# Scores of the samples: even and odd head pairs in different column halves of TensorE

## The reference

```python
logits = jnp.einsum('bthd,btjhd->bthj', q, kg, preferred_element_type=jnp.float32) * ATTN_SCALE
logits = jnp.where(valid[None, :, None, :], logits + bias[None, None], -jnp.inf)
m = jnp.max(logits, axis=-1, keepdims=True)
pr = jnp.exp(logits - m)
den = jnp.sum(pr, axis=-1)
o = jnp.einsum('bthj,btjhd->bthd', pr, vg.astype(jnp.float32)) / den[..., None]
```

## Time and profile before

| what | value |
|---|---|
| median of three runs | 2098.59 us |
| profiled execution | 2098.7 us |
| its span | 2096.9 us |
| mean granted clock of TensorE | 0.987 of 2.4 GHz |
| TensorE busy | 1998.9 us, 95% |
| VectorE busy | 1031.3 us, 49% |
| ScalarE busy | 699.6 us, 33% |
| GpSimd busy | 941.6 us, 45% |

### The profile page before, as it was taken

The page is one execution under the profiler, slowest core; times in us unless marked ns, Lnnn a source line. Parts: engine busy times, 40 slices in busy tenths (PEclk is TensorE's granted clock), DMA queues, the critical chain, the costliest instruction groups (busy, mean ns, idle before and its releaser), DMA issues.

```text
span 2096.9 us, 30132 instructions
## 1 busy us (share of the span) xinstructions
PE 1998.9 (95%) x11992; PEld 1820.7 (87%) x11992; DVE 1031.3 (49%) x1355; ACT 699.6 (33%) x1194; POOL 941.6 (45%) x580
## 2 busy tenths in 40 slices
PE   8999999988888999899999999999999999999999
PEld 7999998777777888565567799999999999999998
DVE  4888803877767666477777561521212212121212
ACT  5344323666556676555552021210010101010010
POOL 4688613777657665234332123233332323232332
PEclk9999999999999999999999999999999999999999
DMA  4444435453343442878755423011111111111112
GB/s 168 149 190 160 149 113 127 115 121 101 87 112 95 117 132 81 267 258 277 232 210 191 172 99 126 31 51 41 51 40 50 40 50 41 49 40 50 40 50 93
DMA packets 117925, 239.36 MB, mean 114 GB/s; under 512 B 29995, under 2 KB 63659, under 8 KB 116284
## 3 DMA queue, kind: packets, MB, share of 16 engines
q1 hardware_dynamic: 94956, 205.69, 30.4%
q10 hardware_dynamic: 22864, 32.25, 4.7%
HBM read 187.78 MB, written 58.67 MB: 118 GB/s over the span
## 4 chain that ended last, share of the span: by engine, by line
PE 65%; DVE 7%; ACT 6%; issue 4%; POOL 1%; DMA 0%; ACTq 0%; DVEq 0%; SPq 0%; POOLq 0%
PE wo_psa L2377 9%; PE wo_psa L2395 9%; PE wo_psb L2377 9%; PE wo_psb L2395 7%; PE dense_ps L966 6%; PE wo_psa L2225 4%; PE sa_s L1512 3%; PE wo_psb L2329 2%; PE wo_psa L2329 2%; DVE att_p L1071 1%; PE att_t_ps L995 1%; ACT att_p L1165 1%; PE ssd_in L1616 1%; PE att_s_ps L984 1%; ACT att_qhi L1182 1%
## 5 line engine op out<-in xcount | busy, mean ns | idle before, releaser
L913 POOL TENSOR_SCALAR att_p<-att_p,att_rden 128x128 f32<-128x128 f32 (+7 forms) x128 | 251.0, 1969 | 132.6 <-DVE att_rden L1053 132.6
L2134 POOL CAST wo_hi<-wo_raw 128x1024 fp32r<-128x1024 f32 x64 | 66.7, 1042 | 496.8 <-issue 242.1
L2492 ACT ACTIVATE r_sq<-stage 128x1056 f32<-128x1056 f32 x32 | 34.8, 1089 | 625.1 <-DVE stage L2693 625.1
L2136 POOL TENSOR_TENSOR wo_lo<-wo_raw,wo_hi 128x1024 fp32r<-128x1024 f32 x64 | 185.3, 2895 | 5.1
L1058 DVE TENSOR_TENSOR att_pTlo<-att_t_ps,att_pThi 128x512 fp32r<-128x512 f32 x192 | 106.3, 554 | 112.1 <-ACT att_pThi L1173 110.6
L2377 PE MATMUL wo_psb<-mix_split,wo_hi 128*128 128x352 f32 x768 | 144.9, 323 | 0.0
L2377 PE MATMUL wo_psa<-mix_split,wo_hi 128*128 128x352 f32 x768 | 144.2, 322 | 0.0
L1173 ACT ACTIVATE att_pThi<-att_t_ps 128x512 fp32r<-128x512 f32 x192 | 93.4, 487 | 127.9 <-PE att_t_ps L995 120.7
L966 PE MATMUL dense_ps<-u_hi,w_hi 128*128 128x352 f32 x480 | 117.8, 347 | 16.4 <-DVE conv_pre L1085 7.8
L2377 PEld LDWEIGHTS wo_psb<-mix_split,wo_hi 128*128 128x128 f32 x768 | 128.3, 188 | 0.5 <-issue 0.5
L2377 PEld LDWEIGHTS wo_psa<-mix_split,wo_hi 128*128 128x128 f32 x768 | 128.0, 188 | 0.0
(11 more groups left out here) (315 smaller groups left out, 5148.0 us busy)
## 6 DMA issues: line engine op xcount, KB each, us to landing
sa_k<-in_cache_k SPq DMA_DIRECT2D x32, 640.0 KB, 7.6
sa_v<-in_cache_v SPq DMA_DIRECT2D x40, 512.0 KB, 4.7
w_raw<-in_w_feat SPq DMA_DIRECT2D x36, 512.0 KB, 6.3
wo_raw<-in_w_up SPq DMA_DIRECT2D x32, 512.0 KB, 3.5
wo_raw<-in_w_down SPq DMA_DIRECT2D x32, 512.0 KB, 3.5
out_qk<-proj_out SPq DMA_DIRECT2D x16, 528.0 KB, 7.9
tmp_bias_rows<-tmp_table ACTq DMA_DIRECT2D x8, 1024.0 KB
att_bias<-tmp_bias_rows SPq DMA_DIRECT2D x16, 512.0 KB, 3.2
```

What stands on the lines that cost most here:

```text
L913: pool.tensor_scalar(slot(h, qt), slot(h, qt), rden[:, qt, :], None, ALU.mult).then_inc(normed, 1)
L2136: pool.tensor_tensor(w_lo[:, j], raw_w, w_hi[:, j].bitcast(F32), ALU.subtract).then_inc(f_split[j], 1)
```

## The change

The two pairs of a group go to different partitions of the same two banks: the even one to partitions 0 to 63 as before, the odd one to 64 to 127. The order within a group becomes columns outside, pairs inside: even 512, odd 512, even 160, odd 160. Each half of the partitions is its own accumulation, begun by the first group's pair and closed by the last group's. VectorE adds the two: first the odd half and the bias go to `probs`, then the old instruction takes the even half and `probs`, writes the sum back and keeps the minimum. `biased` counts twice a sample, and its three waits change with it. Number and size of the matmuls and of the weight loads stay the same.

```diff
-                for i in range(KP):
-                    f = u * KP + i
-                    for c, w in ((0, 512), (512, NKEYS - 512)):
-                        mm = pe.matmul(s_ps[0:R, c:c + w], q_diag[:, f, :], kT[:, u, i, c:c + w],
-                                       start=(f == 0), stop=(f == NPAIR - 1))
+                for c, w in ((0, 512), (512, NKEYS - 512)):
+                    for i in range(KP):
+                        f = u * KP + i
+                        mm = pe.matmul(s_ps[i * R:(i + 1) * R, c:c + w], q_diag[:, f, :], kT[:, u, i, c:c + w],
+                                       start=(f < KP), stop=(f >= NPAIR - KP))
                 mm.then_inc(k_used, 1)
...
-                    pool.wait_ge(biased, b)
+                    pool.wait_ge(biased, 2 * b)
...
-                act.wait_ge(biased, b + 1)
+                act.wait_ge(biased, 2 * b + 2)
...
-                dve.tensor_tensor_reduce(out=probs[:, 0:NKEYS], in0=s_ps[0:R, 0:NKEYS], in1=bias[:], scale=1.0, scalar=3e38,
-                                         op0=ALU.add, op1=ALU.min, accum_out=low[:]).then_inc(biased, 1)
+                dve.tensor_tensor(probs[:, 0:NKEYS], s_ps[R:2 * R, 0:NKEYS], bias[:], ALU.add).then_inc(biased, 1)
+                dve.wait_ge(biased, 2 * b + 1)
+                dve.tensor_tensor_reduce(out=probs[:, 0:NKEYS], in0=s_ps[0:R, 0:NKEYS], in1=probs[:, 0:NKEYS], scale=1.0,
+                                         scalar=3e38, op0=ALU.add, op1=ALU.min, accum_out=low[:]).then_inc(biased, 1)
```

## The result

The changed kernel takes 2110.84 us (median of 12 runs, 2096.31 to 2121.31), the kernel before beside it 2098.51 us (median of 12). The ratio is 1.0054, with an interval of 1.0030 to 1.0078: slower, by 0.3 to 0.8%. The forecast of 2096.8 us said no change, and its range ended at 2107. The profiled execution took 2110.1 us, its span is 2108.3. Over the twelve runs the time goes with the mean granted clock: the fastest of them had 0.982, the slowest 0.972.

What follows compares the result with a forecast made beforehand. The prediction took TensorE (PE), busy 95%, as the bound, with VectorE deciding after the change. Samples 2 to 7 gain 6 x 0.15 = 0.9 us, sample 1 gains 1.0: 1.9 off 2098.7 gives 2096.8 us, range 2092 to 2107.

Steps and rivals of the forecast that it cites:

- step 4: `states(n,1)` on PE, samples 2 to 7: waits for VectorE until 935.24, 0.16 early; afterwards all follows PE, 0.15 us arrive.
- The clock: Rival, chance 0.05: PE's new idle time in the mixers lowers the clock to 1.2 GHz, 1.2 us a sample, 2107.
- the sign of being wrong: Period of samples 2 to 7 moving by more than 0.6 us from 29.2, or score groups staying at 2.40 us.
- Overlap: Score matmuls on PE: even and odd halves run side by side, a group takes 1.75 us, gaining 0.65.
- The sum over 1.56: Score group's halves on PE: only neighbours of unlike parity pair up, 0.43 + 0.43 + 0.43 + 0.27 = 1.56 us.
- The add: VectorE's new instruction before the minimum: 0.85 us plus 0.03 wait, 0.88; hidden in sample 0, not in samples 1 to 7.
- the first rival: No overlap, chance 0.19: PE gains nothing, VectorE's add makes `states(n,1)` 0.46 late, 7 x 0.46 = 3.2, 2101.9 us.
- Step 2: VectorE before y's second turn: GpSimd's earlier decay holds `mix(n,2)`, run ends 0.37 later, turn 0.62 early instead of 1.95.
- Steps 3 and 4: VectorE's new add puts `add_state(n,0)` at 935.17 for 934.91; `states(n,1)` waits for it; 0.15 us a sample arrive.
- A reading: Mixers' stage before the change: the windows of samples 1 to 6 are 29.2 us each.
- PE's gain arrives: Rival, chance 0.07: VectorE isn't in the way of PE's faster scores, 7 x 2.6 = 18.2 us gained, 2080.4.

Runs made afterwards that it cites:

- experiment 3: The change with matmuls of constants filling PE's idle time: two before y's second turn, one each before second state update and first score group, six at stage start; 2095.65 us, 0.9973.
- experiments 5: The change with only some of experiment 3's fillers: rounds only 0.9964, start only 1.0047, second turn of y only 1.0113, second state update only 0.9993.
- experiment 6: The kernel before, matmuls untouched, with three redundant VectorE adds (672, 672 and 256 columns) ahead of the minimum; 2138.35 us, ratio 1.0166.
- experiment 1: The kernel before with one redundant VectorE add ahead of the minimum; 2105.02 us, ratio 1.0016.
- experiment 8: experiment 3 with one filler instead of two at y's second turn, and GpSimd's state decay held until VectorE is through `split_v(n,1)`; 2088.76 us, ratio 0.9947.
- experiment 7: The change with three of four `split_v` moved on VectorE's list behind what PE waits for, 2077.29 us, 0.9881; the same list in the kernel before, 2102.32 us, 1.0001.
- experiment 4: The change with the old order within a score group, pairs outside and columns inside; 2112.17 us, ratio 1.0039.

## Why the prediction was wrong

**The step that failed** is the last half sentence of step 4, "From there all follows PE", which took PE at 2.4 GHz to the end of the sample. It was the rival "The clock", with a chance of 0.05 and 1.2 us a sample. In the seven rounds it took 16 us (219.0 against experiment 3's 203.0), 2.3 a round, and they are 31.3 us on the mean for 29.2, beyond the 0.6 that the prediction itself set as the sign of being wrong. Its "Against" was the error: gaps of 1.32 us at 1.00 were read as if a gap's length told all. The gap at the first score group and the one at the second state update are of like length; the second follows the short matmuls of `inner`, and it alone brings the long falls, in most rounds that have it (experiments 5, 6). That its place behind those short matmuls is the reason was not tried; shown is which gap does it. Nor was the fall short: I worked out a price from one window at 0.74, and the pieces at 0.50 last up to 10.2 us. The rival's sum also adds its loss (7 x 1.2) to 2098.7, where the forecast's gain of 1.9 belongs in it: by its own terms it is 2105, not 2107.

The rest, by the prediction's own steps:

- **Overlap** was right, its size too small: 1.35 us a group for 1.75. The sum over 1.56, by neighbours of unlike parity, failed: all halves of the odd pairs run beside even ones, 4 x 0.43 / 2 + 4 x 0.135 / 2 = 1.13 and the entry. As the prediction said, a larger overlap changes nothing further down, save that PE idles longer: 2.05 and 1.50 us for the forecast 1.3 and 1.1 at these two places.
- **The add**, 0.88 us: 0.89 from its start to the minimum's. Bare, it costs 0.46 a round (experiment 1), as the first rival had it.
- **Step 2**, the held `mix(n,2)` at 1.7 to 2.2 us: 1.82. What it delays was put too high. The stretch from the round's start to the end of `add_skip(n-1,0)` is 9.73 us (920.60 to 930.33) for 9.65 (919.06 to 928.71), 0.08 more and not 0.37: the step lets GpSimd's decay take 2.25 us (922.15 to 924.4), a length that stands in no row, and it took 1.90. The Trainium skill (SBUF — State Buffer, SBUF: two separate sides) has the shared ports as a lock: the one of a VectorE instruction with two inputs in SBUF and a GpSimd one that starts first blocks the other. The trace agrees, with 1.82 us beside GpSimd's instruction and 0.63 once that comes later (experiment 8). In the kernel before it was GpSimd's that was long, 2.39 us beside a `mix(n,2)` of 0.63; the two start 0.01 us apart there, too near to show which was first.
- **Steps 3 and 4**: `states(n,1)` waits for L1897, as forecast. With the clock kept, a round of 2 to 7 is 0.26 us shorter (28.96 for 29.22) where 0.15 was forecast, round 1 0.6 shorter for 1.0, and all seven 2.2 for 1.9. That the sum is so near is partly luck: step 2 was 0.29 too high, and 0.19 of that is lost between the second turn and `states(n,1)`, which comes 16.08 us after the round's start for the forecast 16.18 and 16.34 before.
- **A reading**: not all windows of samples 1 to 6 are 29.2 us. The one from 1006.7 to 1036.2 is 29.5; the sum doesn't use it.
- **PE's gain arrives** (0.07) had the right place to look: it does, once VectorE is out of the way (experiment 7).

**Open.** Why the gap ahead of the second state update brings the clock down in most rounds and not in all, and the longer one ahead of the turn seldom. Why round 0 takes anything from 34 to 43 us, with a low clock, in changed and unchanged kernels (33.8 in experiment 4, 43.2 in experiment 1). And experiment 3 is 5.7 us ahead of the kernel before by its ratio, where its rounds 1 to 7 show 2.2; the rest isn't placed.

## What to carry to other kernels

Where a change makes TensorE faster than the engine that it waits for, the gain turns into idle time, and idle time has a price of its own: read the granted clock of the stage, not of the kernel. Here a new gap of 1.5 us was costly at one place and one of 2 us cheap at another, so length alone doesn't say which. Before or with such a change, look at the late engine's list for work that nobody waits for yet; here moving three instructions turned +0.5% into -1.2%, and the same move without the change gave nothing. To tell clock from waits, fill the gap with matmuls that nobody needs: if the kernel gets faster with more work, it was the clock. One gap at a time can mislead: filling only the cheap one made it slower (2123.53 us).

## What the runs showed of the hardware

- Two float32 matmuls of 64 columns each, in the two halves of the array, run wholly side by side: 1.35 us for a group's eight halves against 2.44, in loads that go in pairs. They needn't be neighbours in the program. The Trainium skill (TensorE: Matmul & The Clock Gate, Part 3: Packing small matmuls — row/col tiling) says that matmuls start and end in program order; with each pair's two halves issued in turn that would keep much of the overlap out, and the trace doesn't agree: 1.36 us in that order, with the four halves of 512 columns ahead of all those of 160 (experiment 4).
- A gap of 1.5 us brought 6.8 to 10.2 us at 1.2 GHz, with TensorE busy throughout (6.80 of 6.80 us in experiment 6): in all seven rounds there, in six of seven with the turn filled, in all four of the change that have it and in four of five of experiment 4. One of 2.05 in another place gave 3.4 or none.
- One filler matmul of 0.86 us in that gap is worth 13 us over the kernel (ratio 0.9993 for 1.0054).
- VectorE's addition of 64 x 672 out of PSUM takes 0.86 us, as long as the minimum of the same size, and the minimum behind it, which reads the other half of the same banks' partitions, 0.85 for 0.84 before.
